# Attention with probabilities halved in row order and turned by DMA, two steps to a slot

## The reference, cut to what matters

```python
s = einsum(q, k) * 64 ** -0.5 + bias            # 128 queries x 384 keys, masked to |distance| <= 128
m = maximum(max(s), sink)
p = exp(s - m)
p = p / (sum(p) + exp(sink - m))
o = einsum(p, v)                                # per block and head; then o * silu(gate)
```

## Time and profile before

| | us |
|---|---|
| median of 3 runs | 2345.09 |
| lowest and highest | 2344.50, 2346.41 |
| the profiled execution | 2344.97 |
| its span, first to last instruction | 2343.0 |
| attention steps, first scores to last `gated` | 1692.3 to 1990.7 |

### The profile page before, as it was taken

The page is one execution under the profiler, slowest core; times in us unless marked ns, Lnnn a source line. Parts: engine busy times, 40 slices in busy tenths (PEclk is TensorE's granted clock), DMA queues, the critical chain, the costliest instruction groups (busy, mean ns, idle before and its releaser), DMA issues. The chain is left out here.

```text
span 2343.0 us, 35223 instructions
## 1 busy us (share of the span) xinstructions
PE 2264.8 (97%) x13534; PEld 1165.1 (50%) x13534; DVE 1458.6 (62%) x2401; ACT 1124.1 (48%) x2179; POOL 876.7 (37%) x673
## 2 busy tenths in 40 slices
PE   8999999998998999999999998999999999999998
PEld 4555555543444445454454554444655555444443
DVE  6999999977555245545445446678377776245323
ACT  7766666686763334334344334333266665333211
POOL 2988888878895111111102010444033333000000
PEclk9999999999999999999999999999999999999999
DMA  5011110033334400100000012223200000102232
GB/s 210 28 45 46 46 46 24 28 119 124 125 119 157 90 2 6 55 1 23 37 1 6 1 55 81 82 90 108 73 10 14 16 1 1 41 19 97 74 108 90
DMA packets 54301, 134.71 MB, mean 57 GB/s; under 512 B 5423, under 2 KB 25519, under 8 KB 53112
## 3 DMA queue, kind: packets, MB, share of 16 engines
q1 hardware_dynamic: 54136, 132.46, 17.1%
HBM read 96.65 MB, written 35.80 MB: 57 GB/s over the span
## 5 line engine op out<-in xcount | busy, mean ns | idle before, releaser
L1178 DVE SCALAR_TENSOR_TENSOR cv_tap_sum<-cv_glu,cv_prm,cv_tap_sum 128x1024 f32<-128x1024 f32 x326 | 418.9, 1288 | 11.9 <-ACT cv_tap_sum L666 2.4
L931 POOL TENSOR_TENSOR mixed<-mixed,cv_tap_products 128x1024 f32<-128x1024 f32 x153 | 363.9, 2379 | 78.0 <-ACT cv_tap_products L681 62.5
L100 PE MATMUL cv_proj<-H_hi,cv_w_ga 128*128 128x416 f16 (+1 forms) x640 | 217.2, 339 | 8.2 <-DVE H_lo L1151 8.2
L101 PE MATMUL cv_proj<-H_lo,cv_w_ga 128*128 128x416 f16 (+1 forms) x640 | 217.3, 339 | 0.0
L102 PE MATMUL cv_proj<-H_hi,cv_w_ga 128*128 128x416 f16 (+1 forms) x640 | 217.2, 339 | 0.0
L100 PE MATMUL gm_vr<-gm_wvr_hi,H_hi 128*128 128x512 f16 x512 | 195.1, 381 | 0.0
L101 PE MATMUL gm_vr<-gm_wvr_lo,H_hi 128*128 128x512 f16 x512 | 195.1, 381 | 0.0
L102 PE MATMUL gm_vr<-gm_wvr_hi,H_lo 128*128 128x512 f16 x512 | 195.1, 381 | 0.0
L1860 POOL TENSOR_TENSOR gm_q_inter<-gm_q_rel,gm_block_decays 128x512 f32<-128x512 f32 x16 | 16.7, 1047 | 453.5 <-ACT gm_block_decays L1942 417.6
L681 ACT ACTIVATE cv_tap_products<-cv_glu,cv_prm 128x1024 f32<-128x1024 f32 x138 | 151.6, 1138 | 35.5 <-POOL mixed L931 35.4
L2470 POOL TENSOR_TENSOR at_probs<-at_probs,at_rsum 128x768 f32<-128x768 f32 (+1 forms) x64 | 90.3, 1411 | 165.3 <-DVE at_rsum L2754 165.3
(11 more groups left out here) (461 smaller groups left out, 5718.2 us busy)
## 6 DMA issues: line engine op xcount, KB each, us to landing
cv_w_stage<-conv_w SPq DMA_DIRECT2D x24, 512.0 KB, 3.9
mixed<-gla_w SPq DMA_DIRECT2D x8, 1024.0 KB, 7.8
go_rows<-h_rows SPq DMA_DIRECT2D x16, 512.0 KB, 4.0
h_rows<-go_rows SPq DMA_DIRECT2D x16, 512.0 KB, 2.8
pl_sums_a<-h_rows SPq DMA_DIRECT2D x16, 512.0 KB, 3.5
out<-pl_sums_a SPq DMA_DIRECT2D x16, 512.0 KB, 2.6
cv_tap_products<-gate_z SPq DMA_DIRECT2D x24, 256.0 KB, 4.7
mixed<-xT SPq DMA_DIRECT2D x12, 416.0 KB, 8.6
```

The source lines that it names most:

```text
L100: nc.tensor.matmul(out, w_hi, x_hi, start=first, stop=False)
L101: nc.tensor.matmul(out, w_hi, x_lo, start=False, stop=False)
L931: nc.gpsimd.tensor_tensor(c_unit(U), c_unit(U), prod[:, r % 3, :], ALU.add).then_inc(s_add, 1)
L1178: nc.vector.scalar_tensor_tensor(out=acc_unit(U), in0=window(U, k), scalar=col(U // 2, k), in1=acc_unit(U), op0=ALU.mult, op1=ALU.add).the ...
```

## The change

The division by the row sum and the split into halves now happen in row order, before the transposition, and the transposition is done by DMA on the f16 halves.

- DVE scales the row sum by 1/256 before its reciprocal. ACT's `high(U)` multiplies the exponentials by it and casts to f16 (`rows[0]`). POOL's `divided` makes the same product in f32 in place, and POOL's new `low` subtracts the high half and writes `rows[1]`.
- SP turns each half of each step, 128 partitions x 768 f16 values, by one DMA into `pts`, now a ring of six; both halves count on the semaphore `s_tr` of the ring slot U % 3. `high` and `low` wait until both turns of step U-3 are in, a turn waits until `outputs(U-6)` is done, `outputs(U)` waits for both its turns.
- `probsT`, `evac_probs`, `probs_lo` and the identity matrix go. `p_t` becomes `p_r`, a second buffer for the scores, so that even and odd steps have their own.
- All engines work in 32 slots W of two steps. PE: scores(2W), scores(2W+1), a whole `project` of 24 matmuls (12 in the last group), outputs(2W-4), outputs(2W-3). `biased(U)` waits for `low(U-3)` instead of `probsT(U-3)`. `gated`, `gate`, `q_evac`, `store_hi` and `store_lo` sit at other places of the order. SP's weight loads stand between the turns.

```diff
-        pts = [m.sb("probsT_hi", [P, 2, 2, BAND], F16), m.sb("probsT_lo", [P, 2, 2, BAND], F16)]
+        rows = [m.sb("probs_hi", [P, 3, 2 * BAND], F16), m.sb("probs_lo", [P, 3, 2 * BAND], F16)]
+        pts = [m.sb("probsT_hi", [P, 6, 2 * BAND // P, P], F16), m.sb("probsT_lo", [P, 6, 2 * BAND // P, P], F16)]
         og = m.sb("gated", [P, GROUP])
         nm, sm, ri = (m.sb(x, [P, 3, 2]) for x in ("neg_max", "sum", "rsum"))
...
-        p_s, p_t = m.ps("p_scores", [P, 2, 512]), m.ps("p_probsT", [P, 2, 512])
+        p_s, p_r = m.ps("p_scores", [P, 2, 512]), m.ps("p_scores_odd", [P, 2, 512])
...
             return attn_slot(M, 2 * i + h) if i < 2 else wst[:, h, :]
+
...
+            return p_r[:, T % 2, :]
+
+        def turned(U):
+
+            return 32 * (U // 3 + 1)
...
+                def turn(U, part):
+                    nk = band(U % NBLK)[1]
+                    if part:
+                        sp.wait_ge(s_pl, U + 1)
+                    else:
+                        sp.wait_ge(s_ph, 2 * U + 2)
+                    if U >= 6:
+                        sp.wait_ge(s_pv, U - 5)
+                    sp.dma_start_transpose(pts[part][:, U % 6, 0:2 * nk, :], packed_pair(part, U)).then_inc(s_tr[U % 3], 16)
+                load(1, 0)
+                load(1, 1)
+                for W in range(NW):
+                    if W >= 6 and W % 8 == 6 and W // 8 + 2 < QT:
+                        load(W // 8 + 2, 0)
+                    if W >= 9 and W % 8 == 1 and W // 8 + 1 < QT:
+                        load(W // 8 + 1, 1)
+                    for part in range(2):
+                        for U in (2 * W, 2 * W + 1):
+                            turn(U, part)
...
                 def divided(U):
                     wd = band(U % NBLK)[1] * P
                     s = sb[:, U % 3, :, 0:wd]
-                    pool.wait_ge(s_ri, U + 1)
+                    pool.wait_ge(s_ph, 2 * U + 2)
                     nc.gpsimd.tensor_tensor(s, s, spread(ri[:, U % 3, :], wd), ALU.mult).then_inc(s_pn, 1)
+
+                def low(U):
+                    wd = band(U % NBLK)[1] * P
+                    pool.wait_ge(s_pn, U + 1)
+                    if U >= 3:
+                        pool.wait_ge(s_tr[U % 3], turned(U - 3))
+                    lo, hi = (packed_pair(part, U).rearrange("p (h n) -> p h n", h=2) for part in (1, 0))
+                    nc.gpsimd.tensor_tensor(lo, sb[:, U % 3, :, 0:wd], hi, ALU.subtract).then_inc(s_pl, 1)
 
...
+                for W in range(NW + 4):
+                    if W < NW:
+                        for U in (2 * W, 2 * W + 1):
+                            divided(U)
+                            low(U)
+                    if W % 2 and W >= 5:
+                        store_lo(W // 2 - 2)
...
-                def evac_probs(U):
-
-                    nk = band(U % NBLK)[1]
-                    act.wait_ge(s_pt, U + 1)
...
+                def high(U):
+                    r, wd = U % 3, band(U % NBLK)[1] * P
+                    act.wait_ge(s_ri, U + 1)
+                    if U >= 3:
+                        act.wait_ge(s_tr[r], turned(U - 3))
                     for h in range(2):
-                        nc.scalar.activation(pts[0][:, U % 2, h, 0:nk * P], p_t[:, h, 0:nk * P], ACT.Copy, scale=WS).then_inc(s_pe, 1)
+                        nc.scalar.activation(packed(0, U, h), sb[:, r, h, 0:wd], ACT.Copy, scale=ri[:, r, h:h + 1]).then_inc(s_ph, 1)
...
+                for W in range(NW + 4):
+                    p, n, g, u = step(2 * W)
+                    if u == 0 and 1 <= g <= NU // 4:
+                        gate(g - 1)
+                    if u == 2 and g + 1 < NU // 4:
+                        q_evac(g + 1)
+                    if W < NW:
...
+                        exps(2 * W)
+                        exps(2 * W + 1)
+                        high(2 * W)
+                        high(2 * W + 1)
...
+                    if u == 2 and g >= 2:
+                        store_hi(g - 2)
...
-                    if U:
-                        pe.wait_ge(s_ad, U)
+                    if U >= 2:
+                        pe.wait_ge(s_ad, U - 1)
                     else:
-                        pe.wait_ge(s_zero, 1)
+                        pe.wait_ge(s_zero, U + 1)
...
-                def probsT(U):
-                    pe.wait_ge(s_pn, U + 1)
...
-                    pe.wait_ge(s_pl, 2 * U + 2)
+                    pe.wait_ge(s_tr[U % 3], turned(U))
...
+                for W in range(NW + 2):
+                    if W < NW:
+                        p, n, g, u = step(2 * W)
+                        scores(2 * W)
+                        scores(2 * W + 1)
                         if g + 1 == NU // 4:
-                            job, ks = (p, g, T, 1), range(2 * u, 2 * u + 2)
+                            project(p, g, n // 4, 1, range(2 * u, 2 * u + 4))
+                        elif u == 0:
+                            project((g + 1) // 4, g + 1, (g + 1) % 4, 0, range(KT))
                         else:
...
+                    else:
+                        next_u(W - NW, range(KT))
+                    if W >= 2:
+                        outputs(2 * W - 4)
+                        outputs(2 * W - 3)
...
-                def probs_lo(U):
-                    nk = band(U % NBLK)[1]
...
-                        dve.wait_ge(s_pt, U - 2)
+                        dve.wait_ge(s_pl, U - 2)
...
+                    nc.vector.tensor_scalar(sm[:, r, :], sm[:, r, :], 1.0 / WS, None, ALU.mult).then_inc(s_rs, 1)
+                    dve.wait_ge(s_rs, U + 1)
                     nc.vector.reciprocal(ri[:, r, :], sm[:, r, :]).then_inc(s_ri, 1)
...
+                for W in range(NW + 4):
+                    p, n, g, u = step(2 * W)
+                    if u == 0 and g >= 2:
+                        gated(g - 2)
+                    if W < NW:
+                        biased(2 * W)
+                        maxima(2 * W)
+                        biased(2 * W + 1)
+                        maxima(2 * W + 1)
+                        reciprocals(2 * W)
+                    if u == 2 and g + 1 < NU // 4:
+                        q_lo(g + 1)
+                    if u == 0 and 1 <= g <= NU // 4:
                         gate(g - 1)
...
+                        reciprocals(2 * W + 1)
...
```

More of the change, by code:

```diff
@@ L2408, in attn_mix @@
         s_og, s_hi, s_lo = m.sem("gated"), m.sem("mixed_hi"), m.sem("mixed_lo")
-        s_s, s_pt, s_pv = m.sem("scores_psum"), m.sem("probsT_psum"), m.sem("oT_psum")
+        s_s, s_pv = m.sem("scores_psum"), m.sem("oT_psum")
+        s_tr = [m.sem(f"probs_turned{r}") for r in range(3)]
         s_ad, s_nm, s_ls, s_nsk = m.sem("biased"), m.sem("neg_max"), m.sem("last_block_sink"), m.sem("neg_sink_done")
[L2412 to L2415, removed]
+        s_ex, s_ph, s_pl = m.sem("exp"), m.sem("probs_hi_done"), m.sem("probs_lo_done")
+        s_rs, s_ri, s_pn = m.sem("sum_scaled"), m.sem("rsum"), m.sem("probs_divided")
+        NW = NU // 2
         def step(U):
@@ L2542, in store_hi @@
                     nc.scalar.activation(mixed(g)[0], og[:, :], ACT.Copy).then_inc(s_hi, 1)
-                for U in range(NU + 4):
-                    p, n, g, u = step(U)
-                    if 2 <= U < NU + 2:
-                        evac_probs(U - 2)
-                    if U < NU:
-                        exps(U)
-                        last = p == QT - 1
-                        if n == 10 and not last:
+                for W in range(NW + 4):
[5 more added lines that the diff above has]
+                    if W < NW:
+                        if n == 10 and p < QT - 1:
                             act.wait_ge(s_q, g + 2)
@@ L2602, in _ @@
                 project(0, 0, 0, 0, range(KT))
-                pe.wait_ge(s_c, NCONST)
                 pe.wait_ge(s_vl, NBLK // 4)
@@ L2763, in gated @@
                                                    op0=ALU.mult, op1=ALU.mult).then_inc(s_og, 1)
-                for U in range(NU + 4):
-                    p, n, g, u = step(U)
-                    if U < NU:
-                        biased(U)
-                    if 1 <= U <= NU:
-                        reciprocals(U - 1)
-                    if U < NU:
-                        maxima(U)
-                        if u == 2 and g + 1 < NU // 4:
-                            q_lo(g + 1)
-                    if u == 0 and 0 < U <= NU:
-                        gate(g - 1)
-                    if 2 <= U < NU + 2:
-                        probs_lo(U - 2)
-                    if U < NU:
-                        if U in (NU - 12, NU - 10):
-                            h = (U - (NU - 12)) // 2
-                            dve.wait_ge(s_uh, h + 1)
-                            nc.vector.scalar_tensor_tensor(out=pool_piece(wu[1], h), in0=attn_slot(M, 4 + h), scalar=WS,
-                                                           in1=pool_piece(wu[0], h), op0=ALU.mult, op1=ALU.subtract).then_inc(s_ul, 1)
```

(4 more changed lines are left out.)

89 lines of the change are left out of this document (27 added, 62 removed).

## The result

The changed kernel takes 2390.46 us (median of 4 runs, 2388.98 to 2392.58) against 2344.8 us (4 runs, 2339.91 to 2346.41) of the kernel before, measured beside it: a ratio of 1.0199, 95% interval 1.0181 to 1.0217. It is slower by 46 us; 2306 was forecast, in a range of 2297 to 2345.

What follows compares the result with a forecast made beforehand. PE was taken to bound the kernel, busy 269.72 us of the attention stage's first 270. 2345.0 - 39.7 (60 steps in 230 us, not 269.7) + 0 (stage end) = 2305.3, stated as 2306; range 2297 to 2345.

Steps and rivals of the forecast that it cites:

- The step that failed: Attention stage: `gated`, `gate`, `q_lo` and the splits keep their number, move by up to one slot, and cost nothing.
- PE's slot, 7.6 us: PE's work in an ordinary two-step slot: 9.2 less 1.4 for `probsT` and 0.2 for change-overs, 7.6 us.
- The circle, 7.5 us: Round through three `at_probs` buffers, `biased` to `low`: 7.15 us plus some 0.35 of hand-overs, one round per slot.
- slots 0 and 1: First slots, where PE has no outputs to do: the circle holds PE, inside the mean of 7.65 us.
- 60 steps in 230 us: First scores to those of step 60: 227 us for 30 slots plus 3 for crowded ones, in place of 269.7.
- 39.7 us of gain: Whole gain forecast, all from the first 60 steps: 230 us in place of 269.7.
- The turns: Transposing DMAs on SP's queue: 1 to 1.5 us of queue each, 3 us to land, hidden.
- Rival B: SP's queue or the turning becomes the bound, a turn holding the queue over 2.3 us; 2371 at 2.5; chance 0.18.
- the two estimates that I made from figures of the Trainium skill: Cost of one turn: 7.9 us if six squares are paid one by one, or 0.75 us at 261 GB/s.
- Rival C: DVE and POOL exclude each other, delaying the scaling of the sums: up to 14 us, 2320; chance 0.08.
- The end, 27.6 us: Scores of step 60 to last `gated`: 9.4 us for slot 30 plus 18.2 for the rest, against 28.7 before.
- the 1 us given up: Saving at the stage's end, cancelled against up to 2 us that half clock after PE's wait in slot 30 could cost.

Runs made afterwards that it cites:

- e1: The changed kernel with a ring of two `gated` buffers instead of one: 2314.2 us, ratio 0.9874 to the kernel before.
- e3: The changed kernel with `gated(g - 2)` moved on DVE from the first to the last place of its slot: 2315.4 us, ratio 0.9885 to the kernel before.
- e9: e8 with DVE's `q_lo` and `gate` between `maxima(2W)` and `biased(2W+1)`, and `u_lo` one slot later: 2300.5 us, ratio 0.9825.
- e2: The changed kernel with `store_hi` and `store_lo` at the end of the slot of their `gated`: 2311.4 us, ratio 0.9867 to the kernel before.
- e4: The changed kernel with every high half turned a second time into a buffer that nobody reads: 2393.7 us.
- e5: e2 with all turns doubled, the second ones into a spare buffer: 2410.9 us.
- e10: e9 with DVE's weight split also put between `maxima(2W)` and `q_lo` or `gate`: 2311.6 us.
- e12: e9 with the gate made one slot earlier, on ACT between the two `exps`, on DVE between the two `reciprocals`: 2312.7 us.
- e8: e2 with DVE's scaling of the row sums in the form that also writes an accumulator: 2303.3 us, ratio 0.9842 to the kernel before.

## Why the prediction was wrong

The step that failed is the sentence that "`gated`, `gate`, `q_lo` and the splits keep their number and move by up to one slot: nothing". `gated` waits for `s_hi` and `s_lo` of the group before. In the old order `store_lo` was a POOL instruction with idle time around it. In the new one it is the last of a full slot of POOL, and `gated` the first of DVE's next, and DVE waits there for 6.9 us in every second slot. I listed who waits for the turns, but for the moved `gated` neither what it waits for nor what stands behind it on DVE, which is everything. That one wait costs 73 to 77 us (e1 to e3): the 27 to 31 us by which the change is faster without it, and the 46 us by which it is slower with it.

Point by point:

- PE's slot, 7.6 us: right; undisturbed slots take 7.33 to 7.50.
- The circle, 7.5 us: its terms held but for one. `low` 1.54 to 1.65 (1.65 taken), `divided` 1.47; two `high` take 1.10, where 0.90 to 0.97 was taken from the form that reads PSUM. It did not hold slots 0 and 1 as I had it: they take 6.2 and 6.4 us. What it missed is a second circle, through the one `gated` buffer: `gated`, two each of `biased` and `maxima`, `high`, a full slot of POOL, `store_lo`.
- 60 steps in 230 us: 306.6 as built; 236.8 without the wait, 231.8 with the other scaling too, 227.5 in e9. For the kernel I had in mind the estimate was near: 33 of the 39.7 us of gain are there in e2.
- The turns: 1.2 us of queue, 2.7 us to land, hidden. Rival B fell (e4, and e5 for its price); the result lies within its range of times by accident. Neither of the two estimates that I made from figures of the Trainium skill came out. From the time that the Trainium skill (VectorE: DVE Perf Modes, The three transpose paths) has for one square by DMA I estimated 7.9 us for six paid one by one, and all six land in 2.7. From the 261 GB/s of the Trainium skill (DMA: Bandwidth & Descriptors, Latency and other measured facts) I estimated 0.75 us for a turn, and a turn takes 1.33 us of the queue when turns stand behind each other, 148 GB/s.
- Rival C was given a chance of 0.08 and up to 14 us; its sign, a scaling longer than 0.3 us, is there in the changed kernel, and in e2 the scaling costs 6 to 8 us. The profile before could not show it: it has no such scaling, and none of its eight weight splits ran beside a POOL instruction.
- The end, 27.6 us: 41.9 as built, 31.5 in e2, 31.0 in e9. Here a size was off even without the wait: PE gets the gate 7.55 us into slot 30 of e9 (1919.21 to 1926.76), not 5.5, since ACT lags and begins the gate 4.7 us into the slot; slot 30 takes 13.5 us, not 9.4. Ten matmuls at half clock, 0.43 in place of 0.215 us each, are 2.1 of that.
- The clock outside the last slot was left out: PE without waits kept it (1.00), PE with these waits had 0.90 over the stretch. What that added by itself was not measured apart; it went away with the waits (0.99 in e2).

Without the failed step the same sum would have stood 5 us from e2, 2306 against 2311.4. Part of that is luck: set against the kernel before timed beside it, e2 gains 31 us where 39 were forecast, so the sum was 8 us off; by its trace e2 is 7 us longer in the 60 steps (236.8 for 230) and 3 at the end (31.5 for 28.7, the 27.6 with the 1 us given up).

## What to carry to other kernels

When an instruction is moved in a hand-written order, write down all that it waits for and the place of each releaser in the new order of its own engine, not only what it costs: the last instruction of one engine's slot must not release the first of another's. Then go around every ring that closes through it, single buffers above all, and add the ring up as one did the obvious one. And a place found idle in one trace is free only if what is put there is ready then; e10 and e12 both filled such a gap with a wait.

## What the runs showed of the hardware

- A turn of 128x768 f16 from SBUF to SBUF takes 1.19 us of SP's queue at least and 1.21 to 1.22 at the median (changed kernel), 1.33 from one to the next when they queue (e5), and lands after 2.7 to 2.8 at the median, 6.0 at most (changed kernel, e1, e2, e9).
- DVE's `tensor_scalar` on 128x2 takes 0.16 us alone and up to 1.43 beside POOL (changed kernel, e2); with an accumulator 0.15, and 0.08 for the read-out (e8). A copy of 128x2 takes 0.17 and 1.36 us, a weight split of 128x1024 1.23 and up to 2.35, and POOL's `divided` beside such a split up to 2.45 in place of 1.47 (before, e2, e8).
- PE of the changed kernel waited 2.18 us and then 1.19 us, until 1807.08, and was granted 0.50 from 1807.4 on; it waited 0.93 us more, worked without a wait from 1808.93, and had the full clock again from 1814.2: the matmuls are 0.43 us apart and then 0.215.
